# The second sums of four PSUM parts: copied by ScalarE and added by GpSimd, in place of one addition by VectorE

## The chip, the cores and the metric

The kernel runs on one core of a Trainium2 chip. The metric is the device time of one execution, in microseconds; lower is better. Engines are named TensorE (PE in the profile), VectorE (DVE), ScalarE (ACT), GpSimd (POOL) and SyncE (SP, which here only issues DMAs).

## The reference

A decoder trunk of two layers, on x of 256 rows by 2048 columns in float32. Each layer computes x + gate * Branch(RMSNorm(x) * (1 + scale) + shift), where shift, scale and gate are three parts of silu(c) @ ada_w + ada_b, a vector times a 2048 x 6144 matrix for each layer.

```python
def moba_branch(h, w_in, q_norm_w, k_norm_w, w_out):
    proj = h @ w_in
    q, k, v, z = jnp.split(proj, 4, axis=-1)
    ...
    return (o * jax.nn.silu(z)) @ w_out
```

Layer 0 is attention: q and k are normed and rotated, there are 16 heads of 128, and with 256 rows there is a single block, so that it is plain causal attention. Layer 1 is an mLSTM in 8 heads, with a projection to 16400 columns where layer 0 has 8192. All of it is in float32.

## The kernel before

**Precision and tiling.** Every large product is made of three: weights and activations are each split into a high part (rounded to the matmul's float format, fp32r) and the rest, and TensorE adds hi*hi, hi*lo and lo*hi in PSUM (`three`, lines 1371 to 1375). A *granule* is one load of weights of 512 KB, 128 partitions by 1024 float32: two blocks of 128 rows by 512 columns of the matrix. For each granule SyncE issues one DMA into `raw`, ScalarE rounds it into `w_hi` (`hi`, line 585), VectorE subtracts to get `w_lo` (`lo`, line 863), and TensorE makes 12 matmuls (`granule0`, line 1384). Five slots (LEAD = 5) hold granules in flight: the w_hi of granule c + 5 waits until TensorE has used granule c.

**The order of layer 0.** `ORDER0` lists the granules as (unit, group, r), units being Q, K, V, Z and O, four groups of four heads each, and r the part of the inner dimension, two of 16 blocks each. The normed input h is made in four steps, each when its block of shift and scale is summed. So the opening, 56 granules long (START), can't go through one unit after the other: it does the first parts (r = 0, 1) of many units, then r = 2, 3, and so on. The sums of Z of groups 0, 1 and 2 and of V of group 1 don't stay in a PSUM bank for that time. They are built up in SBUF in *parts*: `parts[0..3]`. All but the last pieces of them are summed in the PSUM pair `mixes[1]` (mix banks 2 and 3), one unit after the other. `Z_COPIES` (line 391) names the places 3, 6, 9 and 13 where ScalarE copies the first piece of each from `mixes[1]` into its part (`z_copy`, line 647). `Z_ADDS` (lines 393 to 395) names the places where VectorE adds a later piece (`z_add`, line 904): the second pieces at 17, 20, 27 and 32, and further ones at 35, 47, 51, 53 and 55. A place i is the index of the granule behind which the work is due.

**Order on each engine.** Each engine has its own queue, written out by hand. In `run` (line 780), for place i ScalarE and VectorE first do the tasks of the table `first` (for them the copies and the adds), then prepare granule i + 5, then do the table of other tasks. `TAKES0` places on VectorE the products that make up the modulation: `take_ada` (line 866) multiplies one 128x1024 tile of ada_w by a column of silu(c) and adds it to `ada_acc`; 16 tiles make one block of shift and scale. TensorE then sums `ada_acc` over the partitions with 8 small fp32 matmuls (`mod_taken`, line 1502), behind granules 10, 21 and 36 for blocks 1, 2 and 3 (`SUM_AFTER`, line 389), into bank mix[3], which is a half of `mixes[1]`. From there `mod_evac` (VectorE) and `h_make` (ScalarE, with `h_rest` on VectorE) make the next part of h.

**What waits for the adds.** On TensorE `claim0` (line 1401) waits before the first matmul into a bank: granule 19 (the first of Z of group 1 in this round) for z_added 1, granule 29 for z_added 3, granule 34 for z_added 4, granule 54 for z_added 7. `sum_free` (line 1691) lets the sums behind granules 21 and 36 wait for z_added 2 and 5.

**GpSimd** (`gpsimd_program`, line 1314) has small work: constants, the power in the norms (`norm_power`), two memsets of `stream` once all of h is made (line 1333), and then three small operations for each group's q and k norms (lines 1338 to 1344).

**Space.** `work` is one SBUF tensor that is used for different things in turn. Its columns 0 to 4095 hold `xn` until the input is transposed, and from `q_evac` on (place 41) `qk_in` and `rot`, the input and output of `rope` (line 961).

Of the kernel before, what the change touches and what calls it, by code (L numbers as in the profile page):

```python
# [121 lines left out]
def build(nc, x, c, norm_w, ada_w, ada_b, att_w_in, att_q_norm, att_k_norm, att_w_out,  # L122
# [12 lines left out]
    with ctx:  # L135
# [86 lines left out]
        v_pad = part(9728, 1024, "p (t n) -> p t n", t=NT)  # L222
        v_of = [v0, v_pad, v0, v0]
        parts = [z0[0], z0[1], z0[2], v_pad]
        xnT = stream[:].rearrange("p t n -> p (t n)").rearrange("p (k s) -> p k s", s=SEQ)

        cv = part(0, 1024, "p (j t) -> p j t", j=4)
# [57 lines left out]
        def sem(name):  # L285
            return ctx.enter_context(nc.semaphore(name))
# [40 lines left out]
            "coef_step", "y_part", "x1_step", "x1_chunk"))  # L327
        stored, stream_zeroed, gate_summed = (sem(n) for n in (
            "stored", "stream_zeroed", "gate_summed"))
        xnT_act, z_copied, z_added, z_ready, xsq_dve, h_full_ready, x1_sum = (sem(n) for n in (  # L330
            "xnT_act", "z_copied", "z_added", "z_ready", "xsq_dve", "h_full_ready", "x1_sum"))
        qk_turned, qk_padded = (sem(n) for n in ("qk_turned", "qk_padded"))
        v1_hi_ready, pT1_hi_ready = (sem(n) for n in ("v1_hi_ready", "pT1_hi_ready"))
        c_in, conv_turned, norm_turned, ada_pe, scale_added = (sem(n) for n in (
# [4 lines left out]
        def wait(eng, sem, value):  # L339

            if not isinstance(value, int) or value > 0:
                eng.wait_ge(sem, value)
# [34 lines left out]
        def turned(n):  # L377
# [12 lines left out]
        SUM_MOD1 = {70: 4, 87: 5, 95: 6, 110: 7}  # L390
        Z_COPIES = ((0, 3), (1, 6), (2, 9), (3, 13))

        Z_ADDS = ((0, 17, z_copied, 1), (1, 20, z_copied, 2), (2, 27, z_copied, 3), (3, 32, z_copied, 4),
                  (0, 35, z_added, 1), (0, 47, z_added, 5), (1, 51, z_added, 2), (2, 53, z_added, 3),
                  (3, 55, z_added, 4))

        X_AGAIN = 147
        SUM_GATE0 = [(129, 3), (130, 2), (148, 3), (149, 2)]
# [25 lines left out]
        def in0(g, u):  # L424

            return (0, 3, 5, 8)[g] + u + 1
# [220 lines left out]
        def z_copy(act, j, c):  # L647

            act.wait_ge(granule_used, c + 1)
            act.activation(parts[j], mixes[1][:], ACT.Copy).then_inc(z_copied, 1)  # L650

        def z_silu(act):

            for g in range(G0 - 1):
                act.wait_ge(z_added, 6 + g)
                act.activation(z0[g], z0[g], ACT.Silu).then_inc(z_ready, 1)

        def q_evac(act, g, c):
            wait(act, s0_done, g)
            qk_evac(act, g, 0, c)  # L660

        def qk_evac(act, g, u, c):
# [137 lines left out]
        def act_program(act):  # L800
            act.dma_start(rows_c, c[0].rearrange("(t p) -> t p", p=P)).then_inc(c_in, 16)
            act.dma_start(const[:], consts[:, 0:C_COS]).then_inc(consts_in, 16)
            act.dma_start(rows_n, norm_w.rearrange("l (t p) -> (l t) p", p=P)).then_inc(c_in, 16)
            act.dma_start(rows_v, mlstm_norm_w[0].rearrange("(t p) -> t p", p=P)).then_inc(rows_in, 16)
            act.dma_start(conv_rows, mlstm_conv_w[0].rearrange("k (j p) -> (k j) p", p=P)).then_inc(rows_in, 16)
            act.wait_ge(consts_in, 16)
            act.activation(mask_b[:], const[:, C_MASK:C_MASK + P], ACT.Copy)
            act.activation(ident_b[:], ident, ACT.Copy).then_inc(masks_ready, 1)
            act.wait_ge(rows_turned, 1)
            act.activation(cond[:], proj[1][0][:, 0:KT], ACT.Silu).then_inc(cond_ready, 1)  # L810
            for q in range(CHUNKS):
                squares(act, 0, q)
            norm_act(act, 0)

            for q in range(UNIT):
                xnT_evac(act, q)
            layer0 = merged(
                {-5: [lambda: h_make(act, 0, 0)], -4: [lambda: h_make(act, 0, 1)]},
                {i: [lambda b=b: h_make(act, 0, 2 * b), lambda b=b: h_make(act, 0, 2 * b + 1)]
                 for i, b in SUM_AFTER.items()},  # L820
                {41: [lambda: q_evac(act, 0, 41)], 43: [lambda: qk_evac(act, 0, 1, 43)],
                 45: [lambda: vz_evac(act, 0, V_, 45, v0)], 51: [lambda: qkT_evac(act, 0)],
                 54: [lambda: exp0(act, 0)], 58: [lambda: pT0_evac(act, 0)], 60: [lambda: z_silu(act)],
                 65: [lambda: y_hi_act(act, 0)], 68: [lambda: gates_hi(act)]},
                *[{GROUP0[g] + 7: [lambda g=g: q_evac(act, g, GROUP0[g] + 7)],
                   GROUP0[g] + 15: [lambda g=g: qk_evac(act, g, 1, GROUP0[g] + 15)],
                   GROUP0[g] + late0(g) + 20: [lambda g=g: qkT_evac(act, g)],
                   GROUP0[g] + late0(g) + 23: ([] if g == 1 else [lambda g=g: vz_evac(act, g, V_, GROUP0[g] + 23, v0)])
                   + [lambda g=g: exp0(act, g)],
                   GROUP0[g] + late0(g) + 27: [lambda g=g: pT0_evac(act, g)]} for g in range(1, G0)],  # L830
                {GROUP0[1] + 35: [lambda: y_hi_act(act, 1)], GROUP0[2] + 34: [lambda: y_hi_act(act, 2)],
                 GROUP0[3] + 31: [lambda: vz_evac(act, 3, Z_, GROUP0[3] + 31, z0[3], ACT.Silu)],
                 GROUP0[3] + 34: [lambda: y_hi_act(act, 3, None, y_hi_last)]},
                {LAST0 + 2 * q + 3: [lambda q=q: squares(act, 1, q)] for q in range(CHUNKS - 1)},
                gate_tasks(lambda bank, b: gate_evac(act, bank, b), SUM_GATE0, 0))
            run(act, hi, 0, 0, NG0, layer0, -LEAD, {i: [lambda j=j, i=i: z_copy(act, j, i)] for j, i in Z_COPIES})
            squares(act, 1, CHUNKS - 1)
            norm_act(act, 1)
            for q in range(4, UNIT):
                h_make(act, 1, q)  # L840

            run(act, hi, 0, NG0, HEAD, merged(
                {8: [lambda: gates_evac(act), lambda: gates_log(act)], 12: [lambda: floor_exp(act)]},
                act_group1(act, 0, 0, NG0),
                gate_tasks(lambda bank, b: gate_evac(act, bank, b), SUM_GATE1, CHUNKS)))
            run(act, hi, 0, NG0 + HEAD, BODY, merged(
                {1: [lambda: y_hi_act(act, G0, 0)]}, act_group1(act, 1, 0, NG0 + HEAD),
                gate_tasks(lambda bank, b: gate_evac(act, bank, b), SUM_GATE1, CHUNKS + 2)))
            with act.Fori(1, H1 - 2) as it:
                run(act, hi, it, NG0 + HEAD, BODY, merged(  # L850
                    {1: [lambda: y_hi_act(act, it + G0, it)]}, act_group1(act, it + 1, it, NG0 + HEAD)))
            it = H1 - 2
            run(act, hi, it, NG0 + HEAD, BODY, merged(
                {1: [lambda: y_hi_act(act, it + G0, it)],
                 34: [lambda: y_hi_act(act, G0 + H1 - 1, H1 - 1, y_hi_last)]},
                act_group1(act, H1 - 1, it, NG0 + HEAD)))
            run(act, hi, 0, NG0 + HEAD + (H1 - 1) * BODY, UNIT - LEAD, {})
# [103 lines left out]
        def rope(dve, g, u):  # L961

            half = HD // 2
            dve.wait_ge(in_evac, in0(g, u))
            wait(dve, rope_done, 2 * g + u)
            if u == 0:
                wait(dve, pv0_done, g)
# [346 lines left out]
        def gpsimd_program(pool):  # L1314
# [15 lines left out]

            norm_power(0)

            pool.wait_ge(h_act, KT)
            pool.memset(stream[:, 0, :], 0.0)
            pool.memset(stream[:, 1, :], 0.0).then_inc(out_evac, 2)
# [65 lines left out]
        def claim0(pe, c):  # L1401

            u, g, r = ORDER0[c]
            if c < START:
                pe.wait_ge(h_ready, r + 1)
                for first, sem_, value in ((2, mod_out, 1), (5, z_copied, 1), (8, z_copied, 2), (12, mod_out, 2),
                                           (16, z_copied, 4), (19, z_added, 1), (24, mod_out, 3), (29, z_added, 3),
                                           (34, z_added, 4), (46, mod_out, 4), (48, in_evac, in0(0, Q_)),
                                           (52, in_evac, in0(0, K_)), (54, z_added, 7)):
                    if c == first:  # L1410
                        pe.wait_ge(sem_, value)
            elif u == O_:
# [7 lines left out]
            elif r == 0:  # L1420
                if u >= V_:
                    pe.wait_ge(in_evac, in0(g, u - 2))
                elif g == 1:
                    pe.wait_ge(z_added, 8 + u)
                else:
                    pe.wait_ge(out_evac, (g - 1) * CHUNKS + 1 + u)

# [135 lines left out]
        def pv0(pe, g):  # L1563
            pe.wait_ge(pT0_ready, g + 1)
            if g == 1:
                pe.wait_ge(z_added, 9)
            else:
                pe.wait_ge(in_evac, in0(g, V_))
            v = v_of[g]
# [99 lines left out]
        def pe_program(pe):  # L1669
# [10 lines left out]
            for q in range(UNIT):  # L1680
# [7 lines left out]
            pe.wait_ge(xnT_act, UNIT)  # L1688

            free = [(y_lo_ready, G0 - 1)] * 2 + [(y_lo_ready, G0)] * 2  # L1690
            sum_free = {10: (z_copied, 3), 21: (z_added, 2), 36: (z_added, 5), 70: (y_lo_ready, 1), 87: (pT0_ready, 2),
                        95: (y_lo_ready, 2), 110: (pT0_ready, 3)}
            layer0 = merged(
                {i: [lambda i=i, k=k: sum_behind(pe, *sum_free[i], mod_sum, k)]
                 for i, k in (SUM_AFTER | SUM_MOD1).items()},
                {51: [lambda: turn_qk0(pe, 0, z_added, 6)], 53: [lambda: scores0(pe, 0)],
                 58: [lambda: turn_p0(pe, 0)], 62: [lambda: pv0(pe, 0)], 65: [lambda: turn_y(pe, 0, y0)]},
                *[{GROUP0[g] + late0(g) + 20: [lambda g=g, free_=free_: turn_qk0(pe, g, *free_)],
                   GROUP0[g] + late0(g) + 22: [lambda g=g: scores0(pe, g)],
# [109 lines left out]
```

## Time and profile before

| | us |
|---|---|
| three runs | 1507.14, 1510.91, 1511.65 |
| median | 1510.91 |
| the profiled execution | 1509.05 |
| its span, first to last instruction | 1507.2 |
| mean granted TensorE clock, share of full | 0.992 |
| VectorE busy | 1103.8 |
| ScalarE busy | 745.4 |
| GpSimd busy | 44.2 |

How to read it: the profile is of one execution, all its times counted from the first instruction. Busy time of TensorE is modelled and comes out somewhat long: a matmul of 128x512 shows 0.39 us, yet they begin 0.23 us apart at full clock. Two instructions of VectorE overlap a little in the records as well, so that the distance from start to start tells what one costs in a queue without pauses. In a timeline the brackets give the idle time before an instruction and what ended it; "issue" there is time in which nothing that the profile shows was waited for.

### The profile page before, as it was taken

Reading aid. Unit: us, or ns where it says so; the run is one execution under the profiler, and the core shown is the slowest. Engines: PE = TensorE matmul, PEld = TensorE weight load, DVE = VectorE, ACT = ScalarE, POOL = GpSimd, SP = SyncE. Lnnn points to the kernel's source line nnn. Section 1 sums busy time; section 2 is a strip of 40 time slices with the busy share of each in tenths; the row PEclk is TensorE's granted clock in tenths of the full one; section 3 lists DMA queues with packets and bytes.
Section 4 is the critical chain, followed back from the end, with each engine's and each line's share of the span. In section 5 each row is a group of like instructions: output and inputs, shape, how many; then the busy total and the mean of one; then the engine's idle time right before and its main releaser. Section 6 shows DMA issues by size and latency. Waiting matters only on the chain.

```text
span 1507.2 us, 19079 instructions
## 1 busy us (share of the span) xinstructions
PE 1455.9 (97%) x6692; PEld 1203.5 (80%) x6692; DVE 1103.8 (73%) x1233; ACT 745.4 (49%) x1002; POOL 44.2 (3%) x80
## 2 busy tenths in 40 slices
PE   5889999999999989999999999999999999999998
PEld 4667878888888867778888888888888888888886
DVE  5989899989898876878766566566566666666656
ACT  4544646454445455554544544544554454554452
POOL 0000110001000000010000000000000000000000
PEclk9999999999999999999999999999999999999999
DMA  9999889998989745798766566556566566566553
GB/s 346 387 386 387 273 283 336 318 336 278 329 299 352 264 124 182 250 325 293 251 188 187 171 193 183 176 185 191 169 194 183 177 189 190 168 193 190 174 182 111
DMA packets 198613, 361.46 MB, mean 240 GB/s; under 512 B 14252, under 2 KB 47492, under 8 KB 198552
## 3 DMA queue, kind: packets, MB, share of 16 engines
q1 hardware_dynamic: 197832, 359.23, 72.1%
q0 software_dynamic: 304, 1.06, 0.2%
q8 instruction: 37, 0.61, 0.2%
q10 hardware_dynamic: 416, 0.37, 0.1%
q14 instruction: 24, 0.20, 0.0%
HBM read 358.51 MB, written 2.11 MB: 239 GB/s over the span
## 4 chain that ended last, share of the span: by engine, by line
PE 86%; DVE 6%; issue 3%; DMA 3%; ACT 2%; SPq 0%; POOL 0%; DVEq 0%; ACTq 0%; POOLq 0%
PE proj L1373 25%; PE proj L1375 25%; PE proj L1374 25%; DVE ada_acc L882 3%; PE mix L1373 2%; DMA raw<-in_att_w_in 2%; PE mix L1375 2%; PE mix L1374 2%; DVE w_lo L863 1%; PE mix L1507 1%; DMA ada_more<-in_ada_w 1%; PE mix L1584 1%; ACT w_hi L585 1%; PE mix L1632 1%; PE mix L1551 1%
## 5 line engine op out<-in xcount | busy, mean ns | idle before, releaser
L585 ACT ACTIVATE w_hi<-raw 128x1024 fp32r<-128x1024 f32 x480 | 507.9, 1061 | 687.6 <-PE proj L1375 583.9
L863 DVE TENSOR_TENSOR w_lo<-raw,w_hi 128x1024 fp32r<-128x1024 f32 x480 | 585.6, 1222 | 354.4 <-ACT w_hi L585 353.7
L1373 PE MATMUL proj<-w_hi,h_hi 128*128 128x512 f32 x1472 | 582.9, 396 | 4.9 <-DVE w_lo L863 3.0
L1375 PE MATMUL proj<-w_hi,h_lo 128*128 128x512 f32 x1472 | 574.4, 390 | 0.0
L1374 PE MATMUL proj<-w_lo,h_hi 128*128 128x512 f32 x1472 | 573.8, 390 | 0.0
L1373 PEld LDWEIGHTS proj<-w_hi,h_hi 128*128 128x128 f32 x1472 | 276.8, 188 | 65.7 <-issue 8.1
L1375 PEld LDWEIGHTS proj<-w_hi,h_lo 128*128 128x128 f32 x1472 | 276.6, 188 | 58.5
L1374 PEld LDWEIGHTS proj<-w_lo,h_hi 128*128 128x128 f32 x1472 | 277.0, 188 | 57.4 <-issue 1.4
L882 DVE SCALAR_TENSOR_TENSOR ada_acc<-ada_raw,cond,ada_acc 128x1024 f32<-128x1024 f32 x147 | 187.6, 1276 | 5.2 <-DMA ada_raw<-in_ada_w 4.1
L1373 PE MATMUL proj<-w_hi,y_hi 128*128 128x512 f32 x320 | 125.9, 394 | 1.3 <-DVE stream L1043 1.3
L1375 PE MATMUL proj<-w_hi,y_lo 128*128 128x512 f32 x320 | 124.6, 389 | 0.0
L1374 PE MATMUL proj<-w_lo,y_hi 128*128 128x512 f32 x320 | 124.5, 389 | 0.0
L1373 PEld LDWEIGHTS proj<-w_hi,y_hi 128*128 128x128 f32 x320 | 60.1, 188 | 14.3 <-DVE stream L1043 1.6
L1374 PEld LDWEIGHTS proj<-w_lo,y_hi 128*128 128x128 f32 x320 | 60.1, 188 | 12.7 <-issue 0.5
L1375 PEld LDWEIGHTS proj<-w_hi,y_lo 128*128 128x128 f32 x320 | 60.1, 188 | 12.6
L1373 PE MATMUL mix<-w_hi,h_hi 128*128 128x512 f32 x128 | 51.7, 404 | 7.5 <-issue 7.5
L1375 PE MATMUL mix<-w_hi,h_lo 128*128 128x512 f32 x128 | 51.2, 400 | 0.0
L1374 PE MATMUL mix<-w_lo,h_hi 128*128 128x512 f32 x128 | 51.1, 399 | 0.0
L1049 DVE TENSOR_TENSOR ada_raw<-proj,gate 128x1024 f32<-128x1024 f32 x32 | 39.0, 1217 | 5.5 <-PE proj L1375 5.5
L1052 DVE TENSOR_TENSOR stream<-ada_raw,stream 128x1024 f32<-128x1024 f32 x32 | 39.2, 1225 | 1.1
L1095 DVE SCALAR_TENSOR_TENSOR work<-work,conv_c 128x256 f32<-128x256 f32 x96 | 39.9, 476 | 0.0
L1373 PEld LDWEIGHTS mix<-w_hi,h_hi 128*128 128x128 f32 x128 | 24.7, 193 | 14.8 <-issue 9.7
(213 smaller groups left out, 954.5 us busy)
## 6 DMA issues: line engine op xcount, KB each, us to landing
raw<-in_mlstm_w_in SPq DMA_DIRECT2D x192, 512.0 KB, 3.7
ada_raw<-in_ada_w SPq DMA_DIRECT2D x160, 512.0 KB, 5.9
raw<-in_att_w_in SPq DMA_DIRECT2D x128, 512.0 KB, 7.2
raw<-in_mlstm_w_in SPq DMA_DIRECT2D x128, 256.0 KB, 3.0
raw<-in_mlstm_w_out SPq DMA_DIRECT2D x64, 512.0 KB, 4.0
raw<-in_att_w_out SPq DMA_DIRECT2D x32, 512.0 KB, 5.9
ada_more<-in_ada_w SPq DMA_DIRECT2D x16, 512.0 KB, 11.4
work<-in_ada_w SPq DMA_DIRECT2D x16, 512.0 KB, 11.3
```

The costliest lines, as they stand in the source:

```text
L585: act.activation(w_hi[:, c % LEAD, :], raw[:, c % LEAD, :], ACT.Copy).then_inc(hi_ready, 1)
L863: dve.tensor_tensor(w_lo[:, c % LEAD, :], raw[:, c % LEAD, :], w_hi[:, c % LEAD, :].bitcast(F32), ALU.subtract).then_inc(lo_ready, 1)
L882: dve.scalar_tensor_tensor(out=sum_, in0=w, scalar=cond[:, t:t + 1], in1=other, op0=ALU.mult, op1=ALU.add).then_inc(ada_tile, 1)
L1049: dve.tensor_tensor(scaled, both[q % 2][:], gate_both(q), ALU.mult).then_inc(out_part, 1)
L1052: dve.tensor_tensor(x_q, scaled, x_q, ALU.add).then_inc(out_evac, 1)
L1095: op = dve.scalar_tensor_tensor(out=cv[:, j, :], in0=src, scalar=w, in1=cv[:, j, :], op0=ALU.mult, op1=ALU.add)
L1373: pe.matmul(out_, a_hi, b_hi, start=start, stop=False, **kw)
L1374: pe.matmul(out_, a_hi, b_lo, start=False, stop=False, **kw)
L1375: return pe.matmul(out_, a_lo, b_hi, start=False, stop=stop, **kw)
L1507: op = pe.matmul(mix[3][:, j:j + 1], ada_acc[:, k % 2, j // 4, j % 4 * P:(j % 4 + 1) * P], ones[:, 0:1], start=True, stop=True)
L1551: pe.matmul(mix[h][:, P:3 * P], q[:, P:SEQ], k, start=True, stop=False, skip_group_check=True)
L1584: op = pe.transpose(mix[2 + f // 2][:, (f % 2) * SEQ + t * P:(f % 2) * SEQ + (t + 1) * P], y[:, t, f * P:(f + 1) * P], ident)
```

## The change

The second pieces (places 17, 20, 27, 32) are no longer added by VectorE. ScalarE copies each of them from `mixes[1]` into one of four scratch areas, `part_again`, columns 0 to 4095 of `work` (`z_copy_again`), and counts it on `z_copied`; GpSimd adds the scratch area to the part (`z_pooled`), in a loop ahead of its two memsets. What waited for the bank now waits for ScalarE's copy: granules 19, 29 and 34 for z_copied 5, 7 and 8, the sum behind 21 for z_copied 6. The later adds of VectorE on a part wait for GpSimd's add of it. Two waits for all four of GpSimd's adds are new, since the scratch areas lie where q and k go: ScalarE's `q_evac` of group 0 (place 41) and VectorE's first `rope`. The counts of z_added drop by four.

```diff
+        part_again = [part(a, 1024, "p (t n) -> p t n", t=NT) for a in (0, 1024, 2048, 3072)]
...
-        Z_ADDS = ((0, 17, z_copied, 1), (1, 20, z_copied, 2), (2, 27, z_copied, 3), (3, 32, z_copied, 4),
-                  (0, 35, z_added, 1), (0, 47, z_added, 5), (1, 51, z_added, 2), (2, 53, z_added, 3),
-                  (3, 55, z_added, 4))
+        Z_AGAIN = ((0, 17), (1, 20), (2, 27), (3, 32))
+        Z_ADDS = ((0, 35, z_pooled, 1), (0, 47, z_added, 1), (1, 51, z_pooled, 2), (2, 53, z_pooled, 3),
+                  (3, 55, z_pooled, 4))
...
+        def z_copy_again(act, j, c):
+            act.wait_ge(granule_used, c + 1)
+            act.activation(part_again[j], mixes[1][:], ACT.Copy).then_inc(z_copied, 1)
...
         def q_evac(act, g, c):
             wait(act, s0_done, g)
+            if g == 0:
+                act.wait_ge(z_pooled, 4)
...
-            run(act, hi, 0, 0, NG0, layer0, -LEAD, {i: [lambda j=j, i=i: z_copy(act, j, i)] for j, i in Z_COPIES})
+            run(act, hi, 0, 0, NG0, layer0, -LEAD, {i: [lambda j=j, i=i: z_copy(act, j, i)] for j, i in Z_COPIES} | {
+                i: [lambda j=j, i=i: z_copy_again(act, j, i)] for j, i in Z_AGAIN})
...
             dve.wait_ge(in_evac, in0(g, u))
+            if g == 0 and u == 0:
+                dve.wait_ge(z_pooled, 4)
...
             norm_power(0)
+            for n, (j, _) in enumerate(Z_AGAIN):
+                pool.wait_ge(z_copied, len(Z_COPIES) + n + 1)
+                pool.tensor_tensor(parts[j], part_again[j], parts[j], ALU.add).then_inc(z_pooled, 1)
             pool.wait_ge(h_act, KT)
...
-                                           (16, z_copied, 4), (19, z_added, 1), (24, mod_out, 3), (29, z_added, 3),
-                                           (34, z_added, 4), (46, mod_out, 4), (48, in_evac, in0(0, Q_)),
-                                           (52, in_evac, in0(0, K_)), (54, z_added, 7)):
+                                           (16, z_copied, 4), (19, z_copied, 5), (24, mod_out, 3), (29, z_copied, 7),
+                                           (34, z_copied, 8), (46, mod_out, 4), (48, in_evac, in0(0, Q_)),
+                                           (52, in_evac, in0(0, K_)), (54, z_added, 3)):
...
-            sum_free = {10: (z_copied, 3), 21: (z_added, 2), 36: (z_added, 5), 70: (y_lo_ready, 1), 87: (pT0_ready, 2),
+            sum_free = {10: (z_copied, 3), 21: (z_copied, 6), 36: (z_added, 1), 70: (y_lo_ready, 1), 87: (pT0_ready, 2),
```

## Rows read from the trace of the kernel before

**Rows 1.** The page, first part: busy us, share of the span, instructions.

```profile
PE 1455.9 (97%) x6692; PEld 1203.5 (80%) x6692; DVE 1103.8 (73%) x1233; ACT 745.4 (49%) x1002; POOL 44.2 (3%) x80
```

**Rows 2.** Stages: stretch, length, busy us of each engine, PEclk, DMA share, GB/s.

```profile
38.00:152.00 114.00, 102.29 (x435) 81.17 (x435) 104.53 (x99) 52.91 (x63) 0.00 (x0) 0.96 1.05 386
152.00:190.00 38.00, 38.00 (x177) 31.74 (x176) 30.82 (x41) 24.15 (x57) 5.53 (x4) 1.00 0.80 258
190.00:228.00 38.00, 36.56 (x178) 30.01 (x177) 37.67 (x42) 17.18 (x29) 4.21 (x2) 1.00 0.88 294
228.00:540.00 312.00, 310.68 (x1532) 259.76 (x1531) 280.75 (x309) 160.96 (x286) 12.83 (x10) 1.00 0.87 308
```

**Rows 3.** Waits of PE from 120 to 540 us: total, times, longest.

```profile
PE mix L1549 <- ACT work L688: 1.4, 1, 1.4
PE proj L1373 <- DVE stream L1043: 1.3, 1, 1.3
```

**Rows 4.** Timeline of PE around 103 us: start, length, instruction, idle before.

```profile
103.12 0.39 PE L1375 MATMUL mix<-w_hi,h_lo 128*128 128x512 f32 x1
106.46 0.47 PE L1373 MATMUL mix<-w_hi,h_hi 128*128 128x512 f32 x1 [2.95 <-issue]
```

**Rows 5.** Timeline of DVE, 101 to 119 us and one row at 160 us.

```profile
103.95 1.27 DVE L882 SCALAR_TENSOR_TENSOR ada_acc<-ada_raw,cond,ada_acc 128x1024 f32<-128x1024 f32 x1
105.15 1.21 DVE L908 TENSOR_TENSOR work<-mix,work 128x1024 f32<-128x1024 f32 x1
106.28 1.21 DVE L863 TENSOR_TENSOR w_lo<-raw,w_hi 128x1024 fp32r<-128x1024 f32 x1
107.41 1.27 DVE L882 SCALAR_TENSOR_TENSOR ada_acc<-ada_more,cond,ada_acc 128x1024 f32<-128x1024 f32 x1
...
112.05 1.23 DVE L863 TENSOR_TENSOR w_lo<-raw,w_hi 128x1024 fp32r<-128x1024 f32 x1 [1.03 <-ACT w_hi L585]
...
114.39 1.22 DVE L908 TENSOR_TENSOR gate<-mix,gate 128x1024 f32<-128x1024 f32 x1
...
116.65 1.28 DVE L882 SCALAR_TENSOR_TENSOR ada_acc<-work,cond,ada_acc 128x1024 f32<-128x1024 f32 x1
...
160.66 1.22 DVE L908 TENSOR_TENSOR work<-mix,work 128x1024 f32<-128x1024 f32 x1
```

**Rows 6.** Timeline of ACT, 103 to 107 us.

```profile
103.48 1.06 ACT L585 ACTIVATE w_hi<-raw 128x1024 fp32r<-128x1024 f32 x1 [1.81 <-DMA raw<-in_att_w_in]
106.18 1.06 ACT L585 ACTIVATE w_hi<-raw 128x1024 fp32r<-128x1024 f32 x1 [1.64 <-DMA raw<-in_att_w_in]
```

**Rows 7.** Timeline of PE: the sums of modulation blocks 2 and 3.

```profile
118.08 1.92 PE L1507 MATMUL mix<-ones,ada_acc 128*128 128x1 f32 x16 [1.54 <-DVE ada_acc L882]
...
162.41 1.84 PE L1507 MATMUL mix<-ones,ada_acc 128*128 128x1 f32 x16
```

**Rows 8.** Line 650: ns min/median/max, first and last start.

```profile
L650 ACT ACTIVATE gate<-mix x2: 1004/1005/1006, 66.4 to 74.5; 128x1024 f32<-128x1024 f32 x2
```

**Rows 9.** Timeline of POOL.

```profile
169.26 1.81 POOL L1334 MEMSET stream<- 128x2048 f32 x1 [150.42 <-ACT work L643]
...
187.95 1.29 POOL L1340 TENSOR_TENSOR stat<-stat,per_hd 128x16 f32<-128x16 f32 x1 [15.13 <-ACT work L671]
189.32 1.08 POOL L1342 TENSOR_TENSOR stat<-stat,eps_c 128x16 f32<-128x16 f32 x1
...
277.78 0.22 POOL L1340 TENSOR_TENSOR stat<-stat,per_hd 128x16 f32<-128x16 f32 x1 [83.48 <-ACT work L671]
```

**Rows 10.** Timeline of DVE beside the second and third of these.

```profile
187.88 1.28 DVE L882 SCALAR_TENSOR_TENSOR ada_acc<-ada_raw,cond,ada_acc 128x1024 f32<-128x1024 f32 x1
189.07 1.24 DVE L863 TENSOR_TENSOR w_lo<-raw,w_hi 128x1024 fp32r<-128x1024 f32 x1
```

**Rows 11.** Stages of 4 us: columns as in rows 2.

```profile
108.00:112.00 4.00, 4.00 (x12) 3.09 (x12) 3.02 (x3) 1.05 (x1) 0.00 (x0) 0.61 1.05 382
112.00:116.00 4.00, 4.00 (x19) 3.27 (x18) 3.95 (x4) 1.08 (x2) 0.00 (x0) 1.00 1.06 381
```

More of the change, by code:

```diff
@@ L329, in build @@
             "stored", "stream_zeroed", "gate_summed"))
-        xnT_act, z_copied, z_added, z_ready, xsq_dve, h_full_ready, x1_sum = (sem(n) for n in (
-            "xnT_act", "z_copied", "z_added", "z_ready", "xsq_dve", "h_full_ready", "x1_sum"))
+        xnT_act, z_copied, z_pooled, z_added, z_ready, xsq_dve, h_full_ready, x1_sum = (sem(n) for n in (
+            "xnT_act", "z_copied", "z_pooled", "z_added", "z_ready", "xsq_dve", "h_full_ready", "x1_sum"))
         qk_turned, qk_padded = (sem(n) for n in ("qk_turned", "qk_padded"))
@@ L650, in z_copy @@
             act.activation(parts[j], mixes[1][:], ACT.Copy).then_inc(z_copied, 1)
+        def z_copy_again(act, j, c):
+            act.wait_ge(granule_used, c + 1)
+            act.activation(part_again[j], mixes[1][:], ACT.Copy).then_inc(z_copied, 1)
         def z_silu(act):
             for g in range(G0 - 1):
-                act.wait_ge(z_added, 6 + g)
+                act.wait_ge(z_added, 2 + g)
                 act.activation(z0[g], z0[g], ACT.Silu).then_inc(z_ready, 1)
@@ L1423, in claim0 @@
                 elif g == 1:
-                    pe.wait_ge(z_added, 8 + u)
+                    pe.wait_ge(z_added, 4 + u)
                 else:
@@ L1565, in pv0 @@
             if g == 1:
-                pe.wait_ge(z_added, 9)
+                pe.wait_ge(z_added, 5)
             else:
@@ L1695, in pe_program @@
                  for i, k in (SUM_AFTER | SUM_MOD1).items()},
-                {51: [lambda: turn_qk0(pe, 0, z_added, 6)], 53: [lambda: scores0(pe, 0)],
+                {51: [lambda: turn_qk0(pe, 0, z_added, 2)], 53: [lambda: scores0(pe, 0)],
                  58: [lambda: turn_p0(pe, 0)], 62: [lambda: pv0(pe, 0)], 65: [lambda: turn_y(pe, 0, y0)]},
```

## The prediction

> **What bounds the kernel now.** I read the page's busy shares first, then the stages, then the opening engine by engine. TensorE is busy for 97% of the span [rows 1]; but this share hides stages with different limits. From 38 to 152 us it is busy 102.3 of 114 us, while the DMA engines are full and move 386 GB/s, and VectorE is busy 104.5 us. From 152 us on TensorE has no gap worth naming: 38 of 38 us, then 310.7 of 312 [rows 2]. Its waits between 120 and 540 us are two, 1.4 and 1.3 us [rows 3]. So a microsecond that TensorE wins or loses in the opening, before the last granule that the loads hold up, goes through to the end.
>
> Where the change cuts in, TensorE's own rows show a stop: its last matmul before it starts at 103.12, the next at 106.46, 2.95 us idle [rows 4]. The label says "issue", but the code at that place is the claim of granule 19 on the sum that VectorE adds out of the bank, and VectorE's row of that add begins at 105.15 and takes 1.21: it ends 0.10 us before TensorE goes on [rows 5]. VectorE was late because it ran without a pause, as the spacing of its rows shows (1.20 for an ada_acc, 1.13 for a w_lo or an add). ScalarE, by contrast, was waiting for loads at that time: 1.81 us idle before 103.48, and its next w_hi 2.70 later [rows 6].
>
> TensorE's second stop ends at 118.08: the sum of modulation block 2, behind granule 21, waited 1.54 us for the last ada_acc of its block, which began at 116.65 and ended at 117.93 [rows 5, 7]. This second stop is where a gain from the first is kept or lost.
>
> **What is taken away and added.** VectorE loses four adds from PSUM at places 17, 20, 27 and 32, 1.13 us of its queue each. ScalarE gets four copies of 128x1024, 1.00 us each by its first four [rows 8]; at the first two places it was idle for a load, at the last two for TensorE (the w_hi and the copy are set free by the same granule, so these w_hi come 1 us later, against the five granules that TensorE has in hand). No DMA is issued or moved. GpSimd gets four adds with both inputs in SBUF. Its queue was waiting for h_act until 169.26 [rows 9], and its two memsets come behind the fourth add, which I expect done by 157 us; the new waits of q_evac (place 41) and of rope fall due only around 178 us. I cost these at nothing; were the cover gone, ScalarE's w_hi queue would stand behind q_evac's wait.
>
> **Step 1, the stop at 103.5.** Granule 17 is done when ScalarE's w_hi before 103.48 is over; the copy fits into the 1.81 us of idle time and ends near 102.7, before granule 18 does. The 2.95 us go. TensorE then finishes granule 21 at about 111.6, as 19 to 21 take about 2.7 each at full clock (12 matmuls, 0.23 apart).
>
> **Step 2, what is late next.** It then waits for the sum's last ada_acc. VectorE has to run, from 105.15: four w_lo and four ada_acc, 4 x 1.13 + 4 x 1.20 = 9.32 us, plus 0.08 for the last one's own length and 0.15 to wake TensorE: 114.70. Before, this same stretch had also two adds (2.26) and a pause of 1.1 us for a w_hi that TensorE's stop had delayed, which makes 118.08. The loads set a floor: w_hi of granules 22 and 23 start at 103.48 and 106.18, so by the same pace that of 25 starts at 111.58; then 1.06 for w_hi, w_lo, ada_acc and the wake-up give about 115.3. So with GpSimd costing nothing TensorE gains 118.1 - 115.3 = 2.8 us.
>
> **Step 3, the unknown: what a GpSimd add does to VectorE.** No add of this size is in the trace. Its nearest rows are GpSimd's 16-column adds. Alone they take 0.22 us; beside VectorE's two-input work they take 1.29 and 1.08, and they end within 0.1 us of the end of the running VectorE instruction [rows 9, 10]. So GpSimd waits for it and gets in between two. VectorE pays too: its w_lo took 1.24 there, 1.21 without [rows 5, 10]. That is 0.03 us for 16 columns; times 64 it is 1.9 for 1024. The other way to it: a memset takes 1.81 for 2048 columns [rows 9], 0.9 for one pass over 1024, so two read passes make 1.8 and three passes, with the write, 2.7. The bounds of one hold are 0 and 2.7; I take 1.8, from the two roads that meet. Both first adds fall where VectorE runs without a pause, so the sum's start is 114.70 + 2 x 1.8 = 118.3: 0.2 us later than before. A gain would need a hold under 1.7.
>
> The Trainium skill, "SBUF — State Buffer", section "Who interferes with whom", says that a VectorE instruction with two SBUF inputs contends with a GpSimd one that reads SBUF, and that the second to issue fully blocks; the trace agrees as far as the 1.29 against 0.22 goes. "GPSIMD Engine Reference" of the Trainium skill, section 3.1, has 4497 ns for such an add of 2048 columns; half of it, 2.25 us as an estimate, would put the start at 119.2, 1.1 us late.
>
> **Step 4, the third and fourth add.** The third hold (near 139 us) is 0.7 us worse than the add removed; TensorE is some eight microseconds behind the w_lo it needs there. The fourth is followed by VectorE's add at 160.66, which ends at 161.88, while TensorE takes up the next sum at 162.41 [rows 5, 7]: about 0.4 us of cover against 0.7, so 0.2 to 0.3 lost.
>
> **Step 5, TensorE's clock.** After each of the two stops the granted clock fell to its lower level: 12 matmuls in 108 to 112 us, mean 0.61, against 19 in the next 4 us at 1.00 [rows 11]. One such stretch costs about 7 matmuls, 1.6 us. With the change the first stop is gone but the second grows to 118.3 - 111.6 = 6.7 us. The stretch after the first was hidden by the second stop; the one after the second was paid in full and stays. A longer stop may bring up to one stretch more, 0 to 1.6; I take 0.6.
>
> **The sum.** 0.2 + 0.2 + 0.6 = 1.0 us slower. The profiled execution took 1509.05 (span 1507.2) and would become 1510.1; the three runs shown are 1507.14, 1510.91 and 1511.65, so from the median 1510.91 it is 1511.9. These runs lie 0.3% apart, 4.5 us, and that is what a measurement can tell from no change.
>
> **Rivals.** (a) GpSimd's reads hardly hold VectorE: the 0.03 us stand for something paid once per instruction, not per column. For it: each small add costs no more than a few hundredths. Against: GpSimd clearly waits for VectorE. Then the 2.8 us of step 2 are kept; the clock moves this by 1.6 either way; I take 2.6 faster: 1508.3. (b) The slower side, one mechanism: VectorE's ada_acc and w_lo stand still for the whole of each add, 2.7 us. Place: the queue before the sum at 118.08. It decides from a hold of 1.7 us on; the price at 2.7 is 2.0 us there, up to 1.2 at the fourth, and a slow-clock stretch more. I take 3.5: 1514.4. To be over 0.3% slower by the start of the sum alone it would need a hold of 3.9. (c) The change doesn't do what it says: the stop at 103.5 is for something else and stays. For it only the label "issue". Then the holds shift the second stop by the same rule, and the time is about 1512.5.
>
> **How the numbers follow.** Forecast 50%, (a) 27%, (b) 18%, (c) 5%. All centres are within 0.3%. Over 0.3% faster is only the far side of (a) with the scatter of a median: 11%. Over 0.3% slower is the far side of (b), with the clock: 12%. The rest, 77%, is no change. The range takes in the low bound of (a), 4.4 us, and the high bound of (b), about 4.7: 1506.5 to 1515.8.
>
> **What would show it.** VectorE: near each of the four GpSimd adds one w_lo or ada_acc of about 3 us, or a gap of 1.8; if all stay at 1.2, rival (a). GpSimd: four adds of 2 to 3.5 us, before its memsets, at about 102.7, 111, 139 and 153. TensorE: no stop near 103.5 (else (c)), a single one of about 6 us in its place before the sum of block 2; the start of that sum, 118.3 against 118.08, is the number to look at. The lower clock should follow that stop only. ScalarE: four more copies of 1.0 us. The prediction is wrong if anything after 165 us moves by other than a constant, above all if VectorE's run between 190 and 228 us, busy 37.7 of 38 us [rows 2], changes its length.

## The result and the profile after

The change makes the kernel slower: 1516.9 us in the median of 10 runs (1513.83 to 1520.07), the kernel before 1509.38 (10 runs, 1507.14 to 1511.65); ratio 1.0044, 95% interval 1.0036 to 1.0052. The profiled execution's span is 1515.1 us where it was 1507.2. The ten runs of the change are spread over 6.2 us, those of the kernel before over 4.5; why is open.

TensorE, around the place of the old stop [rows 4] and at the sum of modulation block 2 and 3 [rows 7], from its timeline (lines are shifted by 16: L1523 was L1507; the last row is cut off by the window at 168 us, so that it shows 13 of its 16 instructions):

```profile
103.12 0.39 PE L1391 MATMUL mix<-w_hi,h_lo 128*128 128x512 f32 x1
103.35 0.39 PE L1389 MATMUL mix<-w_hi,h_hi 128*128 128x512 f32 x1
...
118.97 3.55 PE L1523 MATMUL mix<-ones,ada_acc 128*128 128x1 f32 x16 [7.30 <-DVE ada_acc L892]
...
166.59 1.61 PE L1523 MATMUL mix<-ones,ada_acc 128*128 128x1 f32 x13 [0.80 <-DVE work L918]
```

The stop of 2.95 us is gone. In its place there is one of 7.30 before the sum of block 2, which starts 0.9 us later than before and then takes 3.55 us, not 1.92. The sum of block 3 starts at 166.6, 4.2 later than before, after a new stop of 0.80.

VectorE and GpSimd in the same stretch, where [rows 5] were before (timelines):

```profile
102.85 1.22 DVE L873 TENSOR_TENSOR w_lo<-raw,w_hi 128x1024 fp32r<-128x1024 f32 x1
103.98 3.43 DVE L892 SCALAR_TENSOR_TENSOR ada_acc<-ada_raw,cond,ada_acc 128x1024 f32<-128x1024 f32 x1
107.33 1.22 DVE L873 TENSOR_TENSOR w_lo<-raw,w_hi 128x1024 fp32r<-128x1024 f32 x1
...
113.13 3.36 DVE L892 SCALAR_TENSOR_TENSOR ada_acc<-work,cond,ada_acc 128x1024 f32<-128x1024 f32 x1
...
117.55 1.27 DVE L892 SCALAR_TENSOR_TENSOR ada_acc<-work,cond,ada_acc 128x1024 f32<-128x1024 f32 x1
...
143.36 2.63 DVE L873 TENSOR_TENSOR w_lo<-raw,w_hi 128x1024 fp32r<-128x1024 f32 x1 [0.73 <-ACT w_hi L587]
...
156.96 2.58 DVE L873 TENSOR_TENSOR w_lo<-raw,w_hi 128x1024 fp32r<-128x1024 f32 x1 [1.15 <-ACT w_hi L587]
```

```profile
102.69 3.64 POOL L1347 TENSOR_TENSOR work<-work 128x1024 f32<-128x1024 f32 x1 [83.99 <-ACT work L657]
111.12 4.29 POOL L1347 TENSOR_TENSOR gate<-work,gate 128x1024 f32<-128x1024 f32 x1 [4.79 <-ACT work L657]
142.47 2.44 POOL L1347 TENSOR_TENSOR gate<-work,gate 128x1024 f32<-128x1024 f32 x1 [27.05 <-ACT work L657]
156.06 2.40 POOL L1347 TENSOR_TENSOR work<-work 128x1024 f32<-128x1024 f32 x1 [11.15 <-ACT work L657]
```

One VectorE instruction beside each of the first two adds takes 3.4 us instead of 1.27: it is held for 2.15 (2.09 the second time). The last ada_acc of block 2 begins at 117.55, where it began at 116.65. GpSimd's first add waits out the running w_lo (3.64 in all). The last two begin while VectorE is idle and take 2.4; they hold the w_lo behind them for 1.4 us. VectorE is idle there, 0.73 and 1.15 us, for a w_hi that ScalarE makes only after its copy.

The clock in stages of 4 us (length, busy us of PE, PEld, DVE, ACT, POOL, then PEclk, DMA share, GB/s):

```profile
112.00:116.00 4.00, 0.00 (x0) 0.00 (x0) 4.00 (x3) 1.21 (x2) 3.41 (x1) 0.72 1.05 380
116.00:120.00 4.00, 1.03 (x5) 1.06 (x6) 3.96 (x4) 0.69 (x1) 0.00 (x0) 0.50 1.05 387
120.00:124.00 4.00, 4.00 (x16) 3.71 (x17) 1.42 (x3) 1.18 (x3) 0.00 (x0) 0.50 1.06 389
124.00:128.00 4.00, 4.00 (x12) 3.10 (x11) 3.17 (x3) 3.06 (x7) 0.00 (x0) 0.57 1.05 387
...
168.00:172.00 4.00, 4.00 (x14) 3.28 (x15) 1.64 (x4) 3.02 (x7) 0.00 (x0) 0.57 0.78 254
```

It falls to its lower level during the stop and is back only at the end of the stage from 124 on, and it falls once more near 168, behind the sum of block 3. Before, each of the two stops had a short fall of its own behind it: the first in [rows 11], the second in this row of the kernel before:

```profile
120.00:124.00 4.00, 4.00 (x13) 3.16 (x14) 3.76 (x5) 3.71 (x8) 0.00 (x0) 0.67 1.06 389
```

The account of the 7.9 us of span: 0.9 by the later start of the first sum, 1.6 by that sum at the lower clock (3.55 against 1.92), 0.8 by the matmuls behind it at the lower clock beyond what there was before, 0.8 by the stop before the next sum: together 4.1 of the 4.2 by which that sum is shifted. Behind it come 1.6 more by the second fall of the clock, and 2.1 later, of which 1.3 belong to this execution alone (see e0).

### The profile page after: what moved, and what is told of

Read it like the earlier page. It is cut to its first block, busy times and chain, and to the rows that moved or that the text cites. A ratio compares the mean times of both kernels' runs of the same rounds, so it can differ in the third digit from the quotient of the medians.

```text
span 1515.1 us, 19081 instructions
## 1 busy us (share of the span) xinstructions
PE 1460.9 (96%) x6692; PEld 1207.2 (80%) x6692; DVE 1106.0 (73%) x1229; ACT 749.2 (49%) x1006; POOL 58.8 (4%) x84
## 4 chain that ended last, share of the span: by engine, by line
PE 78%; DVE 9%; issue 4%; DMA 4%; ACT 3%; POOL 1%; SPq 1%; DVEq 0%; ACTq 0%; POOLq 0%
PE proj L1389 23%; PE proj L1391 23%; PE proj L1390 23%; DVE ada_acc L892 4%; DMA raw<-in_att_w_in 3%; DVE w_lo L873 1%; PE mix L1389 1%; PE mix L1390 1%; PE mix L1391 1%; ACT w_hi L587 1%; DMA ada_more<-in_ada_w 1%; PE mix L1523 1%; PE mix L1600 1%; PE mix L1648 1%; ACT h_hi L640 0%
```

## The experiments

My theory after this profile (H in the expectations): GpSimd's adds hold VectorE, and the late sum of block 2 and the lower clock behind its stop make the loss. The rivals: the copies on ScalarE cost it (C), or an add on GpSimd costs the same wherever it stands.

Twelve runs follow: the change again and eleven variants. Most can be read by three numbers, the start of the sums of block 2 and 3 and the median time. One execution gives the starts; they differ by some tenths of a microsecond, in e1 by 0.9, for reasons that lie ahead of the change. "VectorE, scratch" means adds from ScalarE's copies.

| | who adds, where | sum 2 | sum 3 | us |
|---|---|---|---|---|
| before | VectorE from PSUM, 17, 20, 27, 32 | 118.1 | 162.4 | 1509.4 |
| the change | GpSimd | 119.0 | 166.6 | 1516.9 |
| e0 | the same again | 118.8 | 166.5 | 1515.3, one run |
| e1 | VectorE, scratch, old places | 117.8 | 164.2 | 1512.3 |
| e2 | GpSimd, all behind sum 2 | 115.5 | 164.3 | 1513.8 |
| e3 | nobody | 115.6 | 161.3 | 1508.7 |
| e4 | nobody, GpSimd memsets | 115.4 | 161.2 | 1509.0, one run |
| e5 | GpSimd, in quarters | 118.3 | 166.0 | 1515.0, one run |
| e6 | GpSimd, TensorE kept busy | 118.7 | 164.0 | 1512.3 |
| e7 | VectorE, scratch, late; TensorE kept busy | 116.0 | 159.0 | 1507.2 |
| e8 | nobody; TensorE kept busy | 115.0 | 158.2 | 1506.6 |
| e10 | VectorE, scratch, late | 115.3 | 162.3 | 1509.6 |
| e11 | last two GpSimd, first two VectorE | 117.3 | 164.3 | 1513.8 |
| e12 | first two GpSimd, last two VectorE | 119.0 | 165.4 | 1513.8 |

All medians but the single runs are of 7 to 11 runs. The kernel before was run again beside each set: its median was 1509.4 beside the change, 1509.9 beside e1, e2, e3 and e6, 1509.7 beside e0, e4, e5 and e7, and 1510.2 beside e8, e10, e11 and e12. Kernels of different sets are therefore compared by their distances from it; where the distance of the medians and that of the means disagree, both are given, and 1 us or so between two variants isn't clear of the noise.

**e1: the adds back on VectorE.**

```diff
+        def z_add_again(dve, n, j):
+            dve.wait_ge(z_copied, len(Z_COPIES) + n + 1)
+            dve.tensor_tensor(parts[j], part_again[j], parts[j], ALU.add).then_inc(z_pooled, 1)
...
+                {i: [lambda n=n, j=j: z_add_again(dve, n, j)] for n, (j, i) in enumerate(Z_AGAIN)},
...
-            for n, (j, _) in enumerate(Z_AGAIN):
-                pool.wait_ge(z_copied, len(Z_COPIES) + n + 1)
-                pool.tensor_tensor(parts[j], part_again[j], parts[j], ALU.add).then_inc(z_pooled, 1)
```

> The changed kernel with its four adds taken from GpSimd and given to VectorE, from ScalarE's scratch copies, at the old places 17, 20, 27 and 32. ScalarE's four copies and all waits of TensorE on them stay. Theory H (GpSimd's adds hold VectorE, and the late sum of block 2 brings the lower clock): no VectorE instruction over 1.3 us near the adds, no stop of TensorE at 103.5, the sum of block 2 starts at 114.7 + 2 x 1.13 = 117.0 instead of 119.0; the time is 1 to 3 us under the kernel before (1506.5 to 1508.5). Rival C (the copies on ScalarE and the late w_hi behind them cost the time): as slow as the change, about 1517.

1512.27 us, ratio 1.0013 (1.0005 to 1.0022): slower than before, and faster than the change. The copies on ScalarE aren't what costs the change its 7.5 us, but the forecast of a gain was wrong too. The sum of block 2 starts at 117.8; this execution was 0.9 us late before the change's place (the ada_acc that began at 103.95 begins at 104.81), so that the 117.0 is right. But its timeline has a stop before it of 5.31 (the row is cut off by its window; the whole sum takes 3.55):

```profile
117.83 1.41 PE L1525 MATMUL mix<-ones,ada_acc 128*128 128x1 f32 x6 [5.31 <-DVE ada_acc L892]
```

and the clock is at 0.50 from 116 to 124. Freeing the bank early turned two short stops into one long one, and the sum of block 3 starts 1.8 us later than before. This was the first hint that the clock is the larger term.

**e2: GpSimd's adds behind the sum of block 2.**

```diff
+            pool.wait_ge(mod_out, 3)
             for n, (j, _) in enumerate(Z_AGAIN):
```

> The changed kernel, but GpSimd waits for shift and scale of block 2 (mod_out 3) before its first add, so that the first two adds fall behind the sum of block 2 and not before it. Same work, same engines. Theory H: the sum of block 2 starts at about 115.3, the two holds of 2.15 us fall after 118 us where TensorE has five granules in hand, and cost nothing; the fourth add still costs up to 0.8 us at the sum of block 3. Time 1505.5 to 1508.5, faster than both kernels. Rival (an add on GpSimd costs the same wherever it stands, by what it takes from VectorE in all): 1514 to 1517.

1513.84 us, ratio 1.0027 (1.0016 to 1.0038): between the two expectations. The start of the sum of block 2 was as expected (115.53); "cost nothing" was wrong. The timelines of VectorE and TensorE:

```profile
120.51 6.56 DVE L892 SCALAR_TENSOR_TENSOR ada_acc<-ada_raw,cond,ada_acc 128x1024 f32<-128x1024 f32 x2
```

```profile
164.26 1.95 PE L1524 MATMUL mix<-ones,ada_acc 128*128 128x1 f32 x16 [2.64 <-DVE work L918]
```

Two ada_acc take 6.56 us where they took 2.68, and TensorE stands 2.64 us before the sum of block 3 until VectorE's add at place 35 is done. TensorE's five granules in hand cover a late w_lo, but the sum hangs on the end of VectorE's queue itself. So moving the holds moves a part of the loss to the next sum. The rest is won: against the kernel before e2 loses 3.9 us in the median (4.2 in the mean) where the change loses 7.5 (6.6).

**e3 and e4: no adds; memsets in their place.**

```diff
-                pool.tensor_tensor(parts[j], part_again[j], parts[j], ALU.add).then_inc(z_pooled, 1)
+                pool.sem_inc(z_pooled, 1)
```

```diff
...
+                if n < 2:
+                    pool.memset(rope_a[:], 0.0)
+                    pool.memset(rope_b[:], 0.0)
+                pool.memset(part_again[j], 0.0).then_inc(z_pooled, 1)
```

> The changed kernel without GpSimd's four adds; the copies and all counts stay. Left out of the computation: the second pieces of the sums of Z of groups 0 to 2 and V of group 1. Theory H: what is left when a hold costs nothing: the sum of block 2 starts at 115.3, time 1505 to 1508. Rival C (copies): about 1517, as the change.

> The changed kernel with GpSimd's adds replaced by memsets of as many columns or twice as many (3 memsets, 2048 columns, behind each of the first two copies; 1024 columns behind the others). Left out: the second pieces of the four sums. If it is GpSimd's reading of SBUF that holds VectorE, no VectorE instruction is over 1.3 us, and the sum of block 2 starts at 115.3 to 115.6. If GpSimd holds VectorE by writing too, two VectorE instructions near 104 and 113 are 1 to 2 us longer and the sum starts at 117 to 119.

e3: 1508.74, ratio 0.9991 (0.9982 to 1.0000), a little short of the 1505 to 1508 expected; e4: 1509.03 in one run. e3 has all four copies of ScalarE and is as fast as the kernel before or faster, so that the copies alone cost no time. e4's GpSimd wrote 512, 512 and 1024 columns in 0.52, 0.53 and 0.96 us from 102.34 on, beside these instructions of VectorE:

```profile
102.53 1.22 DVE L873 TENSOR_TENSOR w_lo<-raw,w_hi 128x1024 fp32r<-128x1024 f32 x1
103.67 1.28 DVE L892 SCALAR_TENSOR_TENSOR ada_acc<-ada_raw,cond,ada_acc 128x1024 f32<-128x1024 f32 x1
```

No VectorE instruction is longer for these memsets, as one is for every add: it is GpSimd's reading that holds VectorE, not its writing. The floor of step 2, 115.3, is right (115.6 and 115.4). But 2.5 us won at the sum of block 2 are 1.1 at the next: the sum itself takes 3.55 us in e3 too, after a stop of only 2.55.

**e5: each add in four of 256 columns.**

```diff
-                pool.tensor_tensor(parts[j], part_again[j], parts[j], ALU.add).then_inc(z_pooled, 1)
+                for b in range(4):
+                    t, w = b // 2, slice(b % 2 * 256, b % 2 * 256 + 256)
+                    op = pool.tensor_tensor(parts[j][:, t, w], part_again[j][:, t, w], parts[j][:, t, w], ALU.add)
+                op.then_inc(z_pooled, 1)
```

> The changed kernel with each GpSimd add cut into four of 256 columns. The computation is unchanged. If a hold goes by columns read, four holds of about 0.54 us, VectorE instructions of 1.8 us in place of one of 3.4, and the sum of block 2 again at 119.0. If VectorE's wait is a fixed price for each GpSimd instruction, four times 2.15 us for each add, and the sum at 125 or later. If GpSimd gets fewer turns, the adds take far longer than 4 us and VectorE loses less before the sum.

The hold goes by columns. VectorE's timeline has four instructions of 1.75, half a microsecond more than usual, for each of the first two adds, and 4 x 0.5 = 2.0 is the 2.15 of the whole one but for a tenth or two:

```profile
103.53 1.76 DVE L892 SCALAR_TENSOR_TENSOR ada_acc<-ada_raw,cond,ada_acc 128x1024 f32<-128x1024 f32 x1
105.21 1.75 DVE L873 TENSOR_TENSOR w_lo<-raw,w_hi 128x1024 fp32r<-128x1024 f32 x1
106.89 1.75 DVE L892 SCALAR_TENSOR_TENSOR ada_acc<-ada_more,cond,ada_acc 128x1024 f32<-128x1024 f32 x1
108.56 1.76 DVE L873 TENSOR_TENSOR w_lo<-raw,w_hi 128x1024 fp32r<-128x1024 f32 x1
```

Here the two engines take turns, one instruction each. The sum starts at 118.3, 0.5 to 0.7 us earlier than in the change; the time is 1514.95 in one run, as e0's 1515.3.

**e6: the change with TensorE kept at work.**

```diff
             pe.wait_ge(bank_sem, count)
+            if args == (2,):
+                for _ in range(7):
+                    pe.matmul(mix[2][:], ident, const[:], start=True, stop=True)
```

> The changed kernel; TensorE does seven matmuls of 128x512 float32 into mix[2], which nothing reads, before the sum of block 2, about 6.3 us, so that it is not idle while it waits. The computation is unchanged. Theory: the stop of 7.3 us costs two things, 1.0 us by its end (119.04 against 118.08) and the lower clock (the sum in 3.55 instead of 1.92 us, then 12 matmuls at 0.43 instead of 0.23 us apart), some 4 us. Then the time is 3 to 4.5 us below the change's 1516.9, near 1513. Rival (the lower clock comes from elsewhere or is made up for later): 1516.5 to 1517.5.

1512.28 us in the median, ratio 1.0025 (1.0014 to 1.0036). The sum starts at 118.68, hardly earlier, but takes 1.95:

```profile
118.68 1.95 PE L1523 MATMUL mix<-ones,ada_acc 128*128 128x1 f32 x16 [1.18 <-DVE ada_acc L892]
```

Behind it the clock falls for a short stretch only (0.58 from 120 to 124 us, 1.00 from 124 on). The holds and the stop of 0.80 before the sum of block 3 are there as in the change. The sum of block 3 starts 2.5 us earlier than in e0, and the fall near 168 us is not there, so that at the sum near 352 us (before 352.43, e0 358.20, e6 354.04) the loss is 1.6 us where e0 has 5.8: 4.2 less. The times say 5.2 less by the medians and 3.0 by the means, since four of e6's eleven runs took 1514.8 to 1518.3 and the profile is of one of the other seven (1510.8 to 1512.8). So seven matmuls that nothing reads take away between 45 and 72% of the loss, and the clock costs more than the 0.9 us by which the stop ends later. Of the 4.2 us in the trace 1.7 are the fall near 168 us, and why it goes with these matmuls isn't shown.

**e8, e7 and e10: what the clock takes back of a gain.** e8 is e3 with four such matmuls. e10 is e1 with its adds at later places, where VectorE has time; e7 is e10 with the four matmuls. The edit from e1 to e10:

```diff
-                {i: [lambda n=n, j=j: z_add_again(dve, n, j)] for n, (j, i) in enumerate(Z_AGAIN)},
+                {i: [lambda n=n: z_add_again(dve, n, n)] for n, i in enumerate((23, 25, 29, 38))},
```

> The changed kernel without GpSimd's four adds (left out of the computation: the second pieces of the four sums), and with four matmuls of 128x512 float32 of TensorE that nothing reads before the sum of block 2. Theory: the gain that a free GpSimd add would have brought, if the clock did not take it back: the sum of block 2 at 115.4 to 116, of block 3 at 158 to 159, time 1505 to 1507 against 1508.7 without the matmuls. Rival (the clock does not matter here): 1508.3 to 1509.

> A version meant to beat both: ScalarE's copies stay, VectorE makes the four adds from the scratch areas, but later (places 23, 25, 29 and 38 instead of 17, 20, 27 and 32), GpSimd none; and TensorE does four matmuls of 128x512 float32 that nothing reads (3.4 us) before the sum of block 2. The computation is unchanged. Theory: the sum of block 2 starts at 115.4, the clock stays at its upper level, the sum of block 3 starts at 158.5 to 160 instead of 162.4, and the time is 2.5 to 4 us under the kernel before, 1505.5 to 1507. Rival (what is won before the sum of block 2 is lost again by the loads or by VectorE before the sum of block 3): the sum of block 3 at 162 or later, no gain.

> The version with late VectorE adds (places 23, 25, 29, 38), without TensorE's four idle-time matmuls. Theory: the sum of block 2 starts at 115.4 all the same, but after a stop of 3.3 us the clock is on its lower level for 7 us or so, so that the sum takes 3.5 instead of 1.9 us, and the sum of block 3 starts 2 to 3 us later than in the version with them (161 to 162 instead of 159.0); the time is 1.5 to 3 us above 1507.2. Rival (the matmuls do nothing for the time): within 0.7 us of 1507.2.

e8: 1506.63, ratio 0.9974 (0.9965 to 0.9983). e7: 1507.18, ratio 0.9985 (0.9976 to 0.9994), with the whole computation; the gain over the kernel before is 2.5 us in the medians and 2.0 in the means, at or just under the low end of what was expected. e10: 1509.61, ratio 0.9999 (0.9990 to 1.0008). TensorE's sum of block 2 in e10 and e7:

```profile
115.33 3.54 PE L1525 MATMUL mix<-ones,ada_acc 128*128 128x1 f32 x16 [3.38 <-DVE ada_acc L892]
```

```profile
115.99 1.84 PE L1525 MATMUL mix<-ones,ada_acc 128*128 128x1 f32 x16
```

Without the matmuls e10 reaches this sum even earlier, and the next one 3.3 us later (162.3 against 159.0). By the times, each against the kernel before, the matmuls are worth 1.9 us (1.5 in the means) to a program that has the same adds in the same places, and 2.4 (2.6) from e3 to e8. The starts show more than the times, for two reasons: e7 and e8 have a second fall of the clock behind the sum of block 3, worth 1.7 us, that e10 and e3 have not, and e10's profile is of the slowest of its eleven runs. The length of a stop alone doesn't tell the price: by the stages e4's stop of 3.34 us goes with 6.8 us at the lower level and e10's of 3.38 with 10.2. e7 beats both kernels.

**e11 and e12: which of GpSimd's adds cost.** The loop is cut so that GpSimd makes the last two adds (e11) or the first two (e12), the others being VectorE's as in e1.

```diff
+                {i: [lambda n=n, j=j: z_add_again(dve, n, j)] for n, (j, i) in enumerate(Z_AGAIN) if n not in (2, 3)},
...
-            for n, (j, _) in enumerate(Z_AGAIN):
...
+            pool.wait_ge(z_copied, 7)
+            pool.wait_ge(z_pooled, 2)
+            pool.tensor_tensor(parts[2], part_again[2], parts[2], ALU.add).then_inc(z_pooled, 1)
...
```

> ScalarE's four copies; the first two adds by VectorE from scratch at places 17 and 20, the last two by GpSimd. Against the version with all four by VectorE (sum of block 2 at 117.8, of block 3 at 164.2, stop before the latter under 0.3 us, 1512.3 us) this shows what the last two GpSimd adds cost. Theory as forecast: 0.2 to 0.8 us, as a stop before the sum of block 3. Rival (TensorE's five granules cover them in full): no stop, within 0.5 us of 1512.3.

> ScalarE's four copies; the first two adds by GpSimd, the last two by VectorE from scratch. Theory: all that the change costs but the stop of 0.8 us before the sum of block 3 and a fall of the clock behind it: sum of block 2 at 119.0, long stretch of the lower clock, 1514 to 1516. Rival (the last two GpSimd adds are what costs): 1509 to 1511.

1513.80 (ratio 1.0026, 1.0015 to 1.0037) and 1513.78 (1.0026, 1.0015 to 1.0038). By the distances from the kernel before, each pair costs 1.2 us against e1 in the medians (0.9 and 1.0 in the means), hardly clear of the noise, and the two together 5.2 (4.2). In e11 the stop before the sum of block 3 is there:

```profile
164.29 1.95 PE L1534 MATMUL mix<-ones,ada_acc 128*128 128x1 f32 x16 [0.80 <-DVE work L918]
```

e12's 1513.8 is just under the 1514 to 1516 expected. Why the pairs add up to less than the whole is left open. A second fall of the clock near 168 us, 1.7 us in the stages, is in the profiles of the change, of e0 and of e5 and not in those of e11 and e12; but one of the same size is also behind the sum of block 3 in e2, e7 and e8, so that it isn't a mark of the change. It doesn't follow from the stop of 0.80 us either: e6 and e11 have this stop and no such fall. It wasn't tested by itself.

**e0: the change once more.**

> The changed kernel once more, for its profile. Theory H: the same holds (3.4 us for two VectorE instructions near 104 and 113), the same sum start of 119.0 and a long stretch of the lower clock behind it. The stop of 1.1 us at 374 us, before the scores of group 2, behind a small GpSimd operation of 4.67 us, is either a part of the change (then it is here again and the time from 352 to 402 us is 50.7) or one execution's chance (then 49.4, as in the kernel before).

The holds, the start of the sum, the lower clock and the fall near 168 us are there again. In the change's first profile TensorE had one more stop, of 1.14 us, at 374 us. It is not here: from the sum at 352 us of the kernel before (358 here) to the next it takes 49.3 us, as before. In the first profile GpSimd's small operation there took this long:

```profile
364.93 4.67 POOL L1356 TENSOR_TENSOR stat<-stat,per_hd 128x16 f32<-128x16 f32 x1 [77.27 <-ACT work L680]
```

So those 1.3 us are one execution's chance. e0's span is 1513.3 us, 6.1 over that of the kernel before, and the first profile's without the 1.3 is 6.6 over it. The difference of the means is 6.6 as well; that of the medians is 7.5, and no trace shows the rest.

## Why the prediction was wrong

The sign of the likeliest case was right, a slower kernel, but it was forecast as 1.0 us and is 7.5 between the medians (0.50%; 0.44% between the means), outside the range. Its terms, in microseconds:

| | forecast | in the change's trace |
|---|---|---|
| steps 2 and 3: the sum of block 2 starts later | 0.2 | 0.9 |
| step 4: the stop before the sum of block 3 | 0.2 | 0.8 |
| step 5: the clock behind the long stop | 0.6 | 2.4 |
| the fall of the clock near 168 us | not forecast | 1.6 |
| later | 0 | 2.1, of which 1.3 in one execution alone |

**Cover of the copies, and step 1: right in the main.** TensorE goes on at 103.35 without a stop; ScalarE's first copy starts at 101.61 and ends before granule 18 does. The new waits of q_evac and rope cost nothing that shows. Only the copies at the last two places have a price, and it falls on VectorE (step 4).

**Step 2: right.** 114.70 plus twice the hold is 119.0 for the measured 2.15; the sum started at 118.97. Without adds the floor is 115.4 to 115.6, forecast 115.3.

**Step 3: the kind right, the size a sixth short.** 2.15 us against 1.8. That the two roads to 1.8 met was luck: the first hangs on 0.03 us, and VectorE's w_lo without GpSimd vary by nearly as much (1.21 to 1.23 in [rows 5]). e5 shows that it goes by columns, e4 that it is the reading. The Trainium skill, "SBUF — State Buffer", section "Who interferes with whom", has it just so: a VectorE instruction with two SBUF inputs contends with a GpSimd one that reads SBUF, not with one that only writes. The traces agree: 3.43 us for an ada_acc beside an add, and 1.22 and 1.28 us for w_lo and ada_acc beside memsets. The estimate of 2.25 us from the Trainium skill, "GPSIMD Engine Reference", section 3.1, was nearer than my 1.8. This error alone is 0.7 us at the sum.

**Step 4: too small, and incomplete.** A stop of 0.80 us instead of 0.2 to 0.3, with 1.2 us in the median for the last two adds (e11 against e1). I had each hold 0.7 us worse than the add removed. From the ada_acc before each place to the next one VectorE takes 4.57 and 4.94 us, before 3.47 and 3.46: 1.1 and 1.5 worse. The hold itself is only 1.4 us there, about as long as the add it replaces; the rest is the idle time of 0.73 and 1.15 us behind ScalarE's copy, which I had put at nothing. In e12 VectorE's own adds from scratch fall where this idle time was, and it takes 3.46 and 3.76. The reasoning that TensorE's granules in hand cover a hold was true of w_lo and false of the sum, which waits for VectorE's queue directly; e2 showed it most clearly, with 2.64.

**Step 5: this is the step that failed.** I put a longer stop at "0 to 1.6, I take 0.6", taking the low clock as a stretch of fixed size, of which one more could come. In fact the clock fell during the stop and came back only after some 5 us of granules behind the sum. The sum's small matmuls ran in the low clock too, 3.55 us for 1.92, which I had not counted at all; with the granules behind it that is 2.4 us in place of 0.6. A further fall, 1.6 us, came behind the next sum; its cause is open. e6, with the holds left as they were, puts the two together at 4.2 us in the trace and at 3.0 to 5.2 in the times. Also the sentence that the stretch after the first stop "was hidden by the second stop" had a consequence that I didn't draw: two short stops can cost less than one long one, so that removing the first is no gain by itself. e1 shows it, with the first stop gone, no GpSimd add, and 2.3 us more than before. e1 wasn't run with unread matmuls in its stop, so that the clock's share of these 2.3 us is an inference from its trace.

**Rivals.** (a), GpSimd's reads hardly hold VectorE: false, by the rows of VectorE; and its 2.6 us could not have come even then, since e3 brings 1.2. (b), the slower side: its mechanism is the one that took place, at 2.15 between its 1.7 and 2.7; its price of 3.5 us, and the end of the range that hangs on it, were short by the clock. (Its "about 4.7" above the median is 1515.6, not the range's 1515.8; this changes nothing.) (c): false, the stop is gone.

**The sign of being wrong.** Something after 165 us did move by other than a constant, the fall of the clock at 168; it wasn't VectorE's run between 190 and 228 us. From the sum of block 3 to TensorE's stop at 293 us it takes 130.5 us before and, with 1.6 taken off for the fall, 130.7 in e0 and 131.0 in the first profile.

## What to carry to other kernels

Work moved from VectorE to GpSimd takes VectorE's time all the same when GpSimd reads SBUF and VectorE has two SBUF inputs: an add that cost VectorE 1.13 us of its queue cost it 2.15 as a bystander, and 1.4 where it was idle when the add began. When TensorE is released from one wait only to stand in the next, look at the length of the idle stretch that results and at what runs right behind it: here two short stops, of 2.95 and 1.54 us, were cheaper than one of 5.31 (e1), which goes with 10.2 us at the lower level, where each short one was followed by 3.4. Where such a stop can't be closed, a few matmuls into a free bank, which nothing reads, may pay for themselves; here four were worth 1.5 to 2.6 us (e7 against e10, e8 against e3).

## What the runs showed of the hardware that I had not expected

- Small matmuls double too. The 16 instructions of 128x1 in the sum take 1.84 to 1.95 us at the upper clock and 3.42 to 3.55 at the lower one.
- GpSimd doesn't always get the next turn. Its second add took 4.29 us in one execution of the change and 2.36 in the other, with the running VectorE instruction and one more going first in the longer case; and a 16-column operation that takes 0.22 alone and about 1.1 beside VectorE took 4.67 once.
- Matmuls that nobody reads kept the clock up: with seven of them, 6.2 us in all, the stages from 112 to 120 us show 1.00 where the change had 0.72 and 0.50.
